# A decoder trunk on eight cores: each block's mean square issued behind the gate projection of the block ahead, and two tap-weight loads issued later

## The reference, cut to what matters

```python
h = rmsnorm(x, norm_g)                     # x * rsqrt(mean(x*x) + 1e-6) * g
a_val, a_gate, z_a, gb, gc, hb, z_b = jnp.split(jnp.einsum('btd,de->bte', h, w_in), splits, axis=-1)
u = a_val * jax.nn.sigmoid(a_gate)         # group A: 8 heads of 128 channels
ca, new_a = causal_dwconv(u, buf_a, conv_a_w)          # width 31
y_a = jax.nn.silu(head_layernorm(ca + conv_a_b, ln_a_g, ln_a_b)) * jax.nn.silu(z_a)
v = gc * hb                                # group B
cb, new_b = causal_dwconv(v, buf_b, conv_b_w)          # width 3
y_b = gb * cb * jax.nn.silu(z_b)
x = x + jnp.einsum('bte,ed->btd', jnp.concatenate([y_a, y_b], axis=-1), w_out)
```

## Time and profile before

| what | value |
|---|---|
| time, median of 3 runs | 1271.69 us (1271.34 to 1273.74) |
| profiled execution | 1272.57 us |
| its span on the slowest core, core 3 | 1271.0 us |
| spans of the eight cores | 1261.6 to 1271.0 us |
| PE busy | 1188.4 us, 94% |
| DVE busy | 770.9 us, 61% |
| ACT busy | 512.5 us, 40% |
| mean granted PE clock of the eight cores | 0.988 (core 3) to 0.994 |

### The profile page before, as it was taken

The page is one execution under the profiler, slowest core; times in us unless marked ns, Lnnn a source line. Parts: engine busy times, 40 slices in busy tenths (PEclk is TensorE's granted clock), DMA queues, the critical chain, the costliest instruction groups (busy, mean ns, idle before and its releaser), DMA issues.

```text
span 1271.0 us, 23082 instructions; the slowest of 8 cores (1261.6 to 1271.0 us)
## 1 busy us (share of the span) xinstructions
PE 1188.4 (94%) x7706; PEld 630.2 (50%) x7706; DVE 770.9 (61%) x1462; ACT 512.5 (40%) x820; POOL 249.1 (20%) x349
## 2 busy tenths in 40 slices
PE   4899999999999999999889999999999999999985
PEld 1345554554555555554435555455545554555542
DVE  3555466544666666675864556645477657665677
ACT  4667743676321101112446675357632110111154
POOL 0044423244010000000003433314411000000002
PEclk9899999999999999999989999999999999999998
DMA  9777753586154114221236775246623221322128
GB/s 240 161 106 125 118 84 67 85 131 111 22 92 71 34 18 104 34 35 34 31 47 102 131 133 94 53 88 124 106 36 53 48 34 18 50 35 34 18 77 206
DMA packets 98756, 101.27 MB, mean 80 GB/s; under 512 B 34448, under 2 KB 79760, under 8 KB 98576
## 3 DMA queue, kind: packets, MB, share of 16 engines
q1 hardware_dynamic: 76800, 57.56, 23.6%
q0 software_dynamic: 20880, 37.89, 19.1%
q10 hardware_dynamic: 960, 4.34, 1.3%
HBM read 92.93 MB, written 13.37 MB: 84 GB/s over the span
## 4 chain that ended last, share of the span: by engine, by line
PE 72%; DMA 8%; ACT 6%; DVE 5%; issue 4%; SPq 3%; POOL 1%; DVEq 0%; ACTq 0%; POOLq 0%
PE ps L332 65%; DMA rep<-ubuf 6%; PE ps L455 3%; ACT sq L351 2%; SPq L594 2%; DMA x_sb<-xT 1%; PE ps L474 1%; PE ps L340 1%; SPq L284 1%; ACT L502 1%; DVE acc L709 1%; DVE ubuf L620 1%; DVE x_sb L406 1%; PE ps L358 1%; ACT rstd_t L502 1%
## 5 line engine op out<-in xcount | busy, mean ns | idle before, releaser
L332 PE MATMUL ps<-h_sb,wsl 128*128 128x424 bf16 (+1 forms) x4400 | 818.6, 342 | 0.1
L332 PEld LDWEIGHTS ps<-h_sb,wsl 128*128 128x128 bf16 x4400 | 426.0, 98 | 359.2 <-issue 13.6
L332 PE MATMUL ps<-y_sb,wsl 128*128 128x424 bf16 (+1 forms) x1280 | 238.8, 345 | 18.8 <-DVE sz_t L738 5.4
L406 DVE TENSOR_TENSOR x_sb<-x_sb,ps 128x424 f32<-128x424 f32 (+1 forms) x320 | 179.0, 592 | 41.8 <-PE ps L332 26.1
L332 PEld LDWEIGHTS ps<-y_sb,wsl 128*128 128x128 bf16 x1280 | 124.6, 98 | 129.2 <-issue 31.0
L314 POOL DMA_DIRECT2D wsl<-w_in_r x112 | 60.9, 548 | 540.6 <-PE ps L332 470.9
L750 ACT ACTIVATE th_t<-ps 128x424 f32<-128x424 f32 (+1 forms) x80 | 41.8, 523 | 237.6 <-PE ps L332 206.2
L731 ACT ACTIVATE sz_t<-ps 128x424 f32<-128x424 f32 (+1 forms) x80 | 41.9, 523 | 219.7 <-PE ps L332 202.8
L709 DVE SCALAR_TENSOR_TENSOR acc<-ubuf,cw_b_sb,acc 128x424 f32<-128x424 bf16 (+2 forms) x176 | 106.6, 606 | 18.4
L620 DVE SCALAR_TENSOR_TENSOR ubuf<-th_t,ps 128x424 bf16<-128x424 f32 (+1 forms) x80 | 46.2, 579 | 109.7 <-PE ps L332 89.5
L433 POOL TENSOR_TENSOR sq<-usam,hista 128x992 f32<-128x992 bf16 x32 | 60.9, 1902 | 217.0 <-DVE oa_t L620 210.3
(11 more groups left out here) (52 smaller groups left out, 735.6 us busy)
## 6 DMA issues: line engine op xcount, KB each, us to landing
wsl<-w_in_r POOLq DMA_DIRECT2D x112, 256.0 KB, 5.4
rep<-ubuf SPq DMA_DIRECT2D x256, 109.0 KB, 5.0
wsl<-w_out_r POOLq DMA_DIRECT2D x32, 256.0 KB, 4.8
x_sb<-xT SPq DMA_DIRECT2D x16, 424.0 KB, 13.9
y_fm<-x_sb SPq DMA_DIRECT2D x16, 424.0 KB, 5.0
rep<-ubuf SPq DMA_DIRECT2D x128, 47.0 KB, 2.3
hista<-hist_a SPq DMA_DIRECT2D x16, 255.5 KB, 4.5
oa_copy<-sa_orig ACTq DMA_DIRECT2D x2, 1664.0 KB, 13.3
```

Of the source, the lines that this page charges most:

```text
L332: ins = e.matmul(bank(bk, n), lhsT=l_, rhs=r_, start=(i == 0), stop=(i == len(pairs) - 1))
L406: P.op("dve", (lambda e, bk=bk, m=m: e.tensor_tensor(out=x_sb[:, m, c0:c0 + n], in0=x_sb[:, m, c0:c0 + n], in1=bank(bk, n), op=ALU.add)), ...
```

## The change

Three things are edited, all in `first_head`:

- `gproj(1)`, `gproj(2)` and `gproj(3)` now stand ahead of `stats(2)`, `stats(3)` and `stats(4)`; before, each stood behind them.
- The loads of `cw_a` and `cw_b` are issued by ACT behind Ln and Exp of block 2, not behind those of block 0.
- Nothing is added or removed; DVE, POOL and SP have the same lists as before.

```diff
         stats(0)
-        P.op("act", lambda e: e.dma_start(out=cw_a[:], in_=cw_a_d[:, 0]), writes=[cwa_r], chan=ch_c[2])
-        P.op("act", lambda e: e.dma_start(out=cw_b[:], in_=cw_b_d), writes=[cwb_r], chan=ch_c[3])
...
         stats(1)
         rms_apply(0, 1, rs_of[1])
         vz(0)
+        gproj(1)
         stats(2)
         rms_apply(0, 2, rs_of[2])
-        gproj(1)
+        P.op("act", lambda e: e.dma_start(out=cw_a[:], in_=cw_a_d[:, 0]), writes=[cwa_r], chan=ch_c[2])
+        P.op("act", lambda e: e.dma_start(out=cw_b[:], in_=cw_b_d), writes=[cwb_r], chan=ch_c[3])
         vz(1)
         evac(0)
         evac(1)
...
         a_head_prep(0, 0)
+        gproj(2)
         stats(3)
         rms_apply(0, 3, rs_of[3])
-        gproj(2)
         vz(2)
+        gproj(3)
         stats(4)
         evac(2)
         rms_apply(0, 4, rs_of[4], range(4))
-        gproj(3)
         vz(3)
```

## The result

The changed kernel took 1279.39 us (median of five runs, 1278.66 to 1282.60), the kernel before 1271.69 (five runs, 1269.63 to 1274.41). The ratio is 1.0064 with a 95% interval of 1.0043 to 1.0085: slower, by 5.5 to 10.8 us. The direction had been forecast; 1274.5 was too little, and the time lies above the range of 1271.3 to 1277.3.

What follows compares the result with a forecast made beforehand. The prediction took block 4's norm in the first head, hanging on S4, to set the end. On core 3, 4.1 lost less 1.3 gained made 2.8, added to 1271.69: 1274.5 us, range 1271.3 to 1277.3.

Steps and rivals of the forecast that it cites:

- What bounds the kernel: First head: PE is nearly full behind block 4's norm, so gain or loss up to there is carried to the end.
- S4: End of block 4's mean-square matmuls, 51.14 us on core 3 before; the end was said to move with it.
- Block 4's mean square behind gate projection 3: PE must first finish a gate projection fed by DVE: S4 2.55 later, or 4.1 at half rate, which was taken.
- S3: End of block 3's mean-square matmuls, 44.33 us on core 3 before, forecast 43.0.
- Block 3's squares: On ACT: no more wait for block 1's z projection, so these squares start 1.3 us earlier on core 3.
- Block 2's mean square: On PE behind gate projection 1: S2 at 33.9, a gain of 0.2 at full rate, or a loss of 1.3.
- S2: End of block 2's mean-square matmuls, 34.12 us on core 3 before.
- The tap weights: Later loads of cw_a and cw_b: cost 0 to 0.7, taken as 0; no gain from x coming earlier.
- The sum: On core 3: S4's loss of 4.1 less S3's gain of 1.3, so 2.8 us later.
- still behind core 3: Core 6 loses 0.8 + 2.55 or 0.8 + 4.1, ending at 1271.1 to 1272.6, before core 3 ends.
- C: Rival: PE also at half rate at S2, 1.5, and cw_a late, 0.7: 5.0 in all, 1276.7; chance 0.15.

Runs made afterwards that it cites:

- PE kept busy: Changed kernel with two extra matmuls, their result overwritten unread, behind each of gate projection 3's eight; ratio to the kernel before 1.0016.
- the repeat: The changed kernel, unedited, timed again beside the kernel before; ratio 1.0037.

## Why the prediction was half right

*What bounds the kernel.* Right: "the end moves with S4". Over the twelve kernels the mean span follows point L with a slope of 0.95 (a line fitted to the table); single kernels lie up to 2.5 us off it, and the one furthest off is that with PE kept busy.

*Block 4's mean square behind gate projection 3.* Right in mechanism, and inside the two ends: S4 - S3 was to be 9.36 to about 10.9; it is 10.20 on core 3, 10.05 on the mean core (6.70 before). I took half rate, 4.1 more than before; on core 3 it was 3.4. Both rates occur: 2.37 on core 3, 2.98 on core 6, 1.57 on core 5.

*Block 3's squares.* Right on core 3, and there alone: the SiLU at 38.34 waits for nothing, the DMA issues hold the table load back by 0.32, and the squares start at 38.74 instead of 40.03, 1.3 earlier. S3 is 42.73 where 43.0 was forecast. On the mean core the squares start 0.9 later (38.38, before 37.47), on core 6 0.75 later.

*Block 2's mean square.* Half wrong: I took full rate. Core 6 had it (S2 31.54 + 1.59 = 33.13, forecast 33.1), but three of the eight cores, 0, 3 and 5, ran it at half. On core 3 S2 is 34.23 and not 33.9. On the mean core S2 moved from 32.51 to 33.77, and to 33.67 in the repeat, where no core ran it at half: the later S2 is the wait for block 1's norm.

*The tap weights.* No wait, right: L414 starts at 41.31 straight behind its predecessor. "No gain" in the change agrees with S2; but that the same move is worth 1.8 us on its own I had not seen.

*The sum: the step that failed.* The sum took 1.3 off for an earlier S3 and followed core 3 alone: "4.1 - 1.3 = 2.8 later", with core 6 "still behind core 3". That 1.3 was core 3's. On the mean core S3 is 0.8 later (42.48, before 41.67), and 0.8 + 3.35 = 4.2 is what S4 loses. On core 3 itself S4 is 1.8 later, less than the 2.8. It could gain because it had lost before: the last x of its block 2 had landed at 32.1 us (30.8 on the mean core), its gate projection 1 had run at half rate, and ACT had waited 1.54 for z. Core 6 lost 4.6, inside the forecast's own 0.8 + 2.55 to 0.8 + 4.1. A core's place in one execution does not last: core 6 ended at 1267.9 in spite of its loss, core 3 at 1276.8, 5.8 later for 1.8 at S4. What counts is what all eight lose, since the slowest is drawn anew each time. The mean core's 4.2 would have given 1271.69 + 4.2 = 1275.9.

*A term not in the sum.* Behind S4 I priced nothing. Point L lost 5.1 where S4 lost 4.2. In the stage of gate projection 4 and of block 4's value and z the clock fell to 0.50 on four cores before (2, 3, 5 and 6), on all eight in the changed kernel and on all eight in its repeat. Before, point L came 16.83 to 17.14 behind S4 on those four and 15.75 to 16.02 on the others; now it is 17.05 to 17.51. So four more cores at half rate make some 0.6 of the 0.9; the rest is open.

*What is left.* 4.2 + 0.9 = 5.1 would have given 1276.8, still inside the range. Measured were 7.7 in the first pair of medians and 4.2 in the second (1278.2 against 1274.0). The changed kernel's mean span is nearly the same in both (1272.4 and 1272.1), and of the 3.5 between the pairs 2.3 lie in the kernel before. So, as far as it is known, what put the time outside the range is in good part the draw of the slowest core. The traces show what makes a core slow: behind point L PE waited 0 to 13.4 us for `rep`, from core to core over the fourteen profiled executions, and its clock was at 0.50 for 11 to 28 us. A fit to these two takes up 85% of the variance of the time that the cores need behind point L. Core 5 of the changed kernel had 12.0 and 23.6 of them (7.4 and 15.6 before), core 2 only 0.3 and 16.9. On the mean core the wait was 4.8 before, 6.2 in the changed kernel and 5.1 in its repeat, so it can't be put down to the change. That this draw makes up the whole difference is argued, not shown, and why a core waits long for `rep` is open. Of the rivals C came nearest, by its number and not by its mechanism: half rate at S2 happened on three cores and in the repeat on none, late tap weights on none.

## What to carry to other kernels

A matmul that is fed in pieces by another engine should not stand ahead of one whose operands are complete and whose result starts a chain: the queue turns DVE's 4.66 us into a delay of everything behind it. And make the sum on all cores: the slowest core of one execution may be slowest because it has already paid what the change will cost the others. Where an engine idles for one result while another of its inputs is ready, as DVE does here ahead of block 2's product, changing those two is the cheaper edit; here it was worth 1.7 ± 0.4 us of the mean span.

## What the runs showed of the hardware

The granted clock fell to 0.50 in the paced stretch on some cores and not on others in the same execution (core 3 at S4, core 5 not), with the same instructions. Where it fell between S4 and point L in the kernel before, that stretch took 1.1 us longer (16.95 against 15.82, four cores each). 280 KB of loads moved out of the arrival of x made S2 1.0 us earlier on the mean core. The mean spans of the kernel before differ between chips by up to 1.9 us (1266.2 to 1268.05), nearly half of the +4.4 looked for: only pairs from one chip can be compared.
